# Routing of a mixture-of-experts layer: choice from raw logits, squares from the channel layout, first block gathered by a product on the chip

## The reference, cut to what matters

```
xn2    = rmsnorm(x, norm_ffn_w)               # x * rsqrt(mean(x*x) + 1e-6) * w
logits = xn2 @ router                         # 576 x 8
top_v, top_i = top_k(logits, 2)
gw     = softmax(top_v)
y      = sum over the two experts e of gw[e] * ((silu(xn2 @ w1[e]) * (xn2 @ w3[e])) @ w2[e])
out    = rmsnorm(x + y, norm_final_w)
```

## Time and profile before

| | us |
|---|---|
| median of 3 executions | 2856.9 |
| all three | 2844.24, 2856.9, 2858.02 |
| profiled execution, span from first to last instruction | 2850.7 |
| TensorE matmuls busy | 2468.7 (87%) |
| VectorE busy | 1668.5 (59%) |
| ScalarE busy | 1125.7 (39%) |
| GpSimd busy | 360.3 (13%) |
| mean granted TensorE clock, share of full speed | 0.902 |

### The profile page before, as it was taken

One profiled execution on the slowest core, in us unless ns is written; L12 is line 12 of the kernel. 1 busy time (PEld: TensorE's weight loads), 2 busy tenths in 40 slices (PEclk: granted clock), 3 DMA queues, 4 the chain that ended last, 5 costly groups with the idle time before them and its releaser, 6 DMA issues.

```text
span 2850.7 us, 39807 instructions
## 1 busy us (share of the span) xinstructions
PE 2468.7 (87%) x15802; PEld 2095.7 (74%) x15802; DVE 1668.5 (59%) x1990; ACT 1125.7 (39%) x1370; POOL 360.3 (13%) x160
## 2 busy tenths in 40 slices
PE   5996798698779999969977886979599999999993
PEld 5995686334779999969965863349488888888883
DVE  6853765524423122158627655243689898989895
ACT  4441000453222112134420004532577777777773
POOL 2330000000133333313310000002100000000001
PEclk9997888696889999989978986969799999999997
DMA  4220311300022343122203113001799999999993
GB/s 150 78 61 16 127 53 51 121 23 30 31 96 87 106 149 110 61 94 78 69 16 127 53 51 123 22 30 38 309 420 401 380 381 383 381 387 379 384 376 113
DMA packets 115995, 452.28 MB, mean 159 GB/s; under 512 B 12834, under 2 KB 47522, under 8 KB 86370
## 3 DMA queue, kind: packets, MB, share of 16 engines
q1 hardware_dynamic: 110882, 431.92, 41.3%
q0 software_dynamic: 2624, 9.44, 1.0%
q10 hardware_dynamic: 2304, 8.39, 0.7%
HBM read 415.00 MB, written 42.95 MB: 161 GB/s over the span
## 4 chain that ended last, share of the span: by engine, by line
PE 78%; DVE 12%; ACT 4%; issue 2%; DMA 2%; POOL 1%; another core or an unknown queue 1%; DVEq 0%; SPq 0%; ACTq 0%; POOLq 0%; PEldq 0%
PE ps_buf L508 31%; PE ps_buf L2334 12%; PE ps_buf L2338 6%; PE ps_buf L2365 6%; PE ps_buf L1161 3%; PE ps_buf L2371 3%; PE ps_buf L1196 2%; ACT arena L1735 2%; PE ps_buf L1651 2%; PE ps_buf L1685 1%; PE ps_buf L1149 1%; PE ps_buf L1838 1%; DVE h_buf L572 1%; PE ps_buf L2349 1%; DVE xl_buf L576 1%
## 5 line engine op out<-in xcount | busy, mean ns | idle before, releaser
L508 PE MATMUL ps_buf<-xh_buf,whl_buf 128*128 128x288 f32 x3648 | 663.2, 302 | 76.6 <-POOLq L165 40.5
L2456 DVE TENSOR_TENSOR ring_lo<-ring,high_buf 128x2048 fp32r<-128x2048 f32 (+2 forms) x288 | 594.4, 2108 | 51.7 <-ACT high_buf L2412 49.5
L508 PEld LDWEIGHTS ps_buf<-xh_buf,whl_buf 128*128 128x128 f32 x3648 | 549.6, 192 | 89.5 <-issue 65.0
L2412 ACT CAST high_buf<-ring 128x2048 fp32r<-128x2048 f32 (+2 forms) x288 | 503.0, 1764 | 127.2 <-PE ps_buf L2338 69.0
L508 PE MATMUL ps_buf<-xl_buf,whl_buf 128*128 128x288 f32 x1824 | 398.4, 300 | 0.0
L496 POOL TENSOR_TENSOR whl_buf<-arena,whl_buf 128x1024 fp32r<-128x1024 f32 (+1 forms) x114 | 294.1, 2579 | 602.1 <-ACTq L165 601.5
L493 ACT CAST whl_buf<-arena 128x1024 fp32r<-128x1024 f32 (+1 forms) x114 | 124.7, 1094 | 495.5 <-PE ps_buf L508 476.2
L508 PEld LDWEIGHTS ps_buf<-xl_buf,whl_buf 128*128 128x128 f32 x1824 | 299.0, 193 | 0.0
L2334 PE MATMUL ps_buf<-high_buf,xbh_buf 128*128 128x512 f32 (+1 forms) x768 | 289.8, 377 | 5.3 <-ACT high_buf L2412 5.3
L2334 PE MATMUL ps_buf<-high_buf,xbl_buf 128*128 128x512 f32 (+1 forms) x768 | 288.3, 375 | 0.0
L2338 PE MATMUL ps_buf<-ring_lo,xbh_buf 128*128 128x512 f32 (+1 forms) x768 | 196.1, 377 | 0.0
(11 more groups left out here) (519 smaller groups left out, 3395.8 us busy)
## 6 DMA issues: line engine op xcount, KB each, us to landing
ring<-d_moe_up SPq DMA_DIRECT2D x128, 1024.0 KB, 7.5
ring<-d_moe_dn SPq DMA_DIRECT2D x80, 1024.0 KB, 7.4
ring<-d_moe_up SPq DMA_DIRECT2D x64, 768.0 KB, 6.6
arena<-d_w_in SPq DMA_DIRECT2D x54, 512.0 KB, 3.6
arena<-d_w SPq DMA_DIRECT2D x44, 512.0 KB, 3.6
arena<-d_w SPq DMA_DIRECT2D x16, 704.0 KB, 4.0
arena<-d_pages_c SPq DMA_DIRECT2D x64, 128.0 KB, 2.1
cols_buf<-d_w_out SPq DMA_DIRECT2D x16, 512.0 KB, 3.6
```

The source lines that it names most:

```text
L508: last = nc.tensor.matmul(ps_buf[0:rows, b + a_, 0:HALF], w, m[:, a_ * HALF:(a_ + 1) * HALF], start=start, stop=stop)
L2412: ac.copy(high_part(n), ring[:, 2048 * slot:2048 * slot + unit_cols(n % BLOCK_UNITS)])\
L2456: ve.tensor_tensor(low_part(n), ring[:, at:at + unit_cols(n % BLOCK_UNITS)], high_part(n).bitcast(F32), ALU.subtract).then_inc(S("moe_lo"), 1)
```

## The change: what it does

- **Squares.** They are taken from `x` with channels on the partitions: after each addition VectorE squares the group (128 x 576) and, from the second group on, adds it to a running sum `SQ`. TensorE then sums `SQ` over the partitions with a column of ones, five small products into PSUM. VectorE no longer waits for `XT`, and nothing is left after the loop but the last group.
- **Choice.** The two best experts are taken from the logits before the mean of squares is known. The mean is read between the first and the second choice, and the reciprocal comes after both.
- **Expert numbers** are computed ahead of the slots.
- **Queue of SyncE.** The weight stream no longer waits for the scatters. It waits for them ahead of unit 8 of block 0, and loads block 1 there; block 0 is not loaded from HBM at all. `XN` moves to the last slots of the ring, which unit 8 is the first to touch.
- **Block 0** is gathered on the chip. VectorE builds `HOT` (tokens on the partitions, 128 slots along the row; entry `rstd` where the token's smaller slot is that one, else 0), five instructions that read a row of 1 to 128 from PSUM. TensorE multiplies `XT` by `HOT`, 8 groups of channels by 5 tiles of tokens, fp32. VectorE scales and splits the result in two halves; the first products wait for both halves in turn.
- **Gains** (softmax of the two logits) move behind the first four low parts of block 0.

The core of the diff:

```diff
-        xn_tok = put_at("xn_tok", 5 * D, mx)
+        xn_tok = put_at("xn_tok", 5 * D, mr + RING * 2048 - 5 * D)
@@ wo_dve
-                if sets == 2 and c >= 3:
-                    moe_squares_dve(v, c - 3)
+                if sets == 2:
+                    moe_squares_dve(v, c)
...
-            if sets == 2:
-                for k in range(KD - 3, KD):
-                    moe_squares_dve(v, k)
@@ moe_wo_pe
             moe_turn_pe(KD - 1)
+            pe.matmul(ps_buf[:, 0, 256:256 + P], tb("ones"), tb("rwp")[:, P:2 * P], start=True, stop=True)
+            pe.wait_ge(S("moe_squares"), KD)
+            for i, (t0, n) in enumerate(TILES):
+                last = pe.matmul(ps_buf[0:n, 0, 128 + i:129 + i], SQ[:, 1, t0:t0 + n], tb("ones")[:, 0:1], start=True, stop=True)
+            last.then_inc(S("moe_sums"), 1)
@@ moe_squares_dve
-            ve.wait_ge(S("moe_xt"), k + 1)
-            w = XT[:, :, P * k:P * k + P]
-            v(ve.tensor_tensor(sq_buf[:, 0:5 * P].rearrange("p (i c) -> p i c", i=5), w, w, ALU.mult))
-            v(ve.tensor_reduce(sq_part[:, 5 * k:5 * k + 5], sq_buf[:, 0:5 * P].rearrange("p (i c) -> p i c", i=5), AX.X, ALU.add))
+            if k == 0:
+                v(ve.tensor_tensor(SQ[:, 1, :], x[:, k, :], x[:, k, :], ALU.mult), S("moe_squares"))
+            else:
+                v(ve.tensor_tensor(SQ[:, 0, :], x[:, k, :], x[:, k, :], ALU.mult))
+                v(ve.tensor_tensor(SQ[:, 1, :], SQ[:, 1, :], SQ[:, 0, :], ALU.add), S("moe_squares"))
@@ moe_choose_dve, after the first choice
+                if k == 0:
+                    ve.wait_ge(S("moe_sums"), 1)
+                    v(ve.tensor_scalar(mean2[:, 0:4], ps_buf[:, 0, 128:132], 1.0 / D, 1e-6, ALU.mult, ALU.add))
+                    v(ve.tensor_scalar(mean2[0:64, 4:5], ps_buf[0:64, 0, 132:133], 1.0 / D, 1e-6, ALU.mult, ALU.add), S("moe_mean"))
@@ after both choices
+            ve.wait_ge(S("moe_root"), 1)
+            v(ve.reciprocal(rstd_t, rstd_t), S("moe_rstd"))
@@ after the slots
+            v(ve.tensor_tensor(best, slots[:, 0, :], slots[:, 1, :], ALU.min))
+            for i, (t0, n) in enumerate(TILES):
+                v(ve.tensor_scalar(HOT[0:n, i, :], ps_buf[0:n, 0, 256:256 + P], best[0:n, i:i + 1], rstd_t[0:n, i:i + 1],
+                                   ALU.is_equal, ALU.mult), S("moe_hot"))
@@ moe_sp
-                if b == 0:
-                    sp.wait_ge(S("moe_xs"), 16 * 10)
-                    sp.dma_start(XB[:, 0, :], A["xs"][0:P]).then_inc(S("moe_xb_0"), 16)
...
+                    if b == 0 and u == 8:
+                        sp.wait_ge(S("moe_xs"), 16 * 10)
+                        sp.dma_start(XB[:, 1, :], A["xs"][P:2 * P]).then_inc(S("moe_xb_1"), 16)
@@ new
+        def moe_dispatch_pe():
+            pe = nc.tensor
+            pe.wait_ge(S("moe_xt"), KD)
+            pe.wait_ge(S("moe_hot"), 5)
+            for k in range(KD):
+                for i, (t0, n) in enumerate(TILES):
+                    last = pe.matmul(ps_buf[:, k // 4, P * (k % 4):P * (k % 4) + P], XT[0:n, i, P * k:P * k + P], HOT[0:n, i, :],
+                                     start=i == 0, stop=i == 4)
+                if k == 3:
+                    last.then_inc(S("moe_xbT_half"), 1)
+            last.then_inc(S("moe_xbT"), 1)
@@ moe_dve
-            xbt(0)
+            for h in range(2):
+                ve.wait_ge(S("moe_xbT" if h else "moe_xbT_half"), 1)
+                ks = slice(4 * h, 4 * h + 4)
+                v(ve.tensor_tensor(XBT[:, ks], ps_buf[:, h, 0:512].rearrange("p (k t) -> p k t", t=P),
+                                   nffn[:, ks].unsqueeze(2).to_broadcast([P, 4, P]), ALU.mult))
+                v(ve.tensor_copy(XBH[:, 0, ks], XBT[:, ks]))
+                v(ve.tensor_tensor(XBL[:, 0, ks], XBT[:, ks], XBH[:, 0, ks].bitcast(F32), ALU.subtract),
+                  S("moe_xbt" if h else "moe_xbt_half"))
             lows(0, 0, HIGHS)
+            moe_gains_dve(v)
```

More of the change, by code:

```diff
@@ L275, in build @@
         se_buf = put_at("se_buf", 2 * 512, mc + 2 * E1)
-        sq_buf = put_at("sq_buf", D, mc + 2048)
+        sq_buf = put_at("sq_buf", 2 * T, mc + 2048)
+        hot_buf = put_at("hot_buf", 5 * P, mc + 3264)
         xt_buf = put_at("xt_buf", 5 * D, mc + 4096)
@@ L2074, in build @@
         XT = grid(xt_buf, 0, 5, D)
+        SQ = grid(sq_buf, 0, 2, T)
+        HOT = grid(hot_buf, 0, 5, P)
         XN = grid(xn_tok, 0, 5, D)
@@ L2184, in spread5 @@
                 return ap.unsqueeze(2).to_broadcast([P, 5, 8])
[L2186 to L2187 removed]
             v(ve.memset(lg, 0.0))
+            v(ve.memset(mean2, 1.0))
             ve.wait_ge(S("moe_logits"), 1)
@@ L2191, in moe_choose_dve @@
             v(ve.tensor_copy(lg[0:64, 4, :], ps_buf[0:64, 4, 32:40]))
-            ve.wait_ge(S("moe_root"), 1)
-            v(ve.reciprocal(rstd_t, rstd_t), S("moe_rstd"))
             rank = tb("rrank").rearrange("p (i e) -> p i e", i=5)
@@ L2215, in moe_choose_dve @@
             v(ve.tensor_tensor_scan(last_e, tb("ones")[:, 0:8], blocks_e, 0.0, ALU.mult, ALU.add))
+            w = over[0:1, :].rearrange("p (b e) -> p b e", e=8)
+            v(ve.tensor_tensor(w, tb("blocks", 1).rearrange("p (b e) -> p b e", e=8),
+                               last_e[0:1, :].unsqueeze(1).to_broadcast([1, NBK, 8]), ALU.is_ge))
+            v(ve.tensor_reduce(which[0:1, :], w, AX.X, ALU.add))
+            v(ve.tensor_scalar(ebt_buf[:, :], which[0:1, :], 7.0, None, ALU.min), S("moe_experts"))
             v(ve.tensor_tensor(start_e, last_e, blocks_e, ALU.subtract))
@@ L2223, in moe_choose_dve, with moe_gains_dve @@
             v(ve.tensor_scalar(slot_buf[:, 0:10], slots.rearrange("p k i -> p (k i)"), -1.0, None, ALU.add), S("moe_slots"))
[L2224 to L2228, removed]
+            v(ve.tensor_tensor(best, slots[:, 0, :], slots[:, 1, :], ALU.min))
+            for i, (t0, n) in enumerate(TILES):
+                v(ve.tensor_scalar(HOT[0:n, i, :], ps_buf[0:n, 0, 256:256 + P], best[0:n, i:i + 1], rstd_t[0:n, i:i + 1],
+                                   ALU.is_equal, ALU.mult), S("moe_hot"))
+        def moe_gains_dve(v):
+            ve = nc.vector
             ve.wait_ge(S("moe_exp"), 1)
@@ L2287, in moe_sp @@
                 e = sp.value_load(ebt_buf[0:1, b:b + 1], min_val=0, max_val=7)
-                if b == 0:
-                    sp.wait_ge(S("moe_xs"), 16 * 10)
-                    sp.dma_start(XB[:, 0, :], A["xs"][0:P]).then_inc(S("moe_xb_0"), 16)
-                if b + 1 < NBK:
-                    if b:
-                        sp.wait_ge(S("moe_xbT"), b)
+                if b and b + 1 < NBK:
+                    sp.wait_ge(S("moe_xbT"), b)
                     sp.dma_start(XB[:, (b + 1) % 2, :], A["xs"][P * (b + 1):P * (b + 2)])\
@@ L2323, in moe_up_pe @@
             o = 2 * (gi % 2)
-            if g == 0:
+            if g == 0 and b:
                 pe.wait_ge(S("moe_xbt"), b + 1)
@@ L2328, in moe_up_pe @@
             for q in range(2):
+                if gi == 0:
+                    pe.wait_ge(S("moe_xbt_half" if q == 0 else "moe_xbt"), 1)
                 for w in range(2):
@@ L2375, in moe_pe @@
         def moe_pe():
-            moe_xT_pe(0)
+            moe_dispatch_pe()
             for b in range(NBK):
```

7 lines of the change are left out of this document (3 added, 4 removed).

## The result

The changed kernel takes 2836.83 us (median of nine runs, 2829.76 to 2848.49), the kernel before 2850.12 (nine runs, 2841.14 to 2858.02). The ratio is 0.9953, with an interval of [0.9933, 0.9974]: 13.3 us or 0.47% faster. The interval excludes 1, so the kernel is faster, though by a little less than the 0.5% that I had called the limit of what can be told. The forecast was 2840.9, in a range of 2829 to 2851.

A forecast was written before the change was run, and what follows sets the result against it. TensorE bounds the blocks; routing, scatters and a late weight unit fill the hole ahead of them. 17.0 less 0.9 gave 16 us off the span, 2834.7, and 6.2 above that 2840.9; range 2829 to 2851.

The forecast's parts named there:

- HOT: Five VectorE instructions building the gather's matrix: 0.41 each and a gap of 0.03, 2.2 together, ready at 2004.6.
- The squares and the choice: Routing after the logits: copies start 5.5 us earlier, line 2208 5.36 early, first weights asked for at 2001.2.
- The DMA share: Weights and scatters side by side: scatters get a third of 420 GB/s, 140, and weights 280.
- Rival 2: Weights and scatters together reach 350 GB/s, not 420; unit 8 late by 6 to 7 more; gain 9.5, 2847; chance 0.16.
- the gather of block 0: 80 TensorE instructions after HOT: 11.7 us, with ends of 9.6 and 20.0, finished at 2016.4.
- The clock: During the gather, TensorE starts at clock 0.50 and rises after 4 us: 16 instructions in 4.0, 64 in 7.7.
- The first low part: Unit 0's low part on VectorE waits for the split: 2018.25 + 2.29 = 2020.5, its four products ending at 2021.5.
- The term for unit 8: Unit 8's weights, asked for after the scatters, are ready at 2042.6, wanted at 2041.7: 0.9 late.
- the likeliest case: Whole change: gain of 16 us off the span, with a neighbourhood of 13 to 20; chance 0.64.
- Rival 1: The clock does not rise during the gather: 8.3 lost, less 0.9 of unit 8; gain 8.6, 2848; chance 0.13.
- Rival 3: SyncE's wait for slow scatters holds up unit 8: at 6 us per scatter 14 us slower, 2871; chance 0.07.
- Rival 4: The change doesn't do what it says: the sums wait or VectorE's loop falls behind; no price of its own.

The follow-up runs named there:

- e1: The changed kernel without gather and early weights: SyncE waits for the scatters and loads both blocks before the first unit; 2843.52 us, ratio 0.9993.
- e8: The changed kernel with low parts between the split's halves, scatter wait moved to unit 14, 2 and 15 idle products around the count; 2835.56 us, ratio 0.9946.
- e4: The changed kernel with idle TensorE products, 10 ahead of the count and 30 behind it; 2837.98 us, ratio 0.9968.
- r_after: The changed kernel run again with no edit; 2840.1 us, ratio 0.9955.
- e3: The changed kernel with low parts of units 0 and 1 between the split's halves and the gather in other PSUM banks; 2841.13 us, ratio 0.9964.
- e5: e3 with idle TensorE products, 4 before the count and 36 after it; 2842.12 us, ratio 0.996.
- e6: e5 with SyncE's wait for the scatters moved from unit 8 to unit 14 and the scattered rows outside those ring slots; 2836.11 us, ratio 0.9943.
- e2: e1 with units 0 to 7 asked for first and the scatter wait and both block loads ahead of unit 8; 2861.66 us, ratio 1.0042.

## Why the prediction was right, and where its sizes were off

**Right, to a few tenths.** The squares and the choice: the copies at 0.11 after the logits' end (forecast 0.1), the sum of both picks at 3.82 (3.77), the first weights at 8.31 (8.3), the scatters at 9.79 (9.6). By e1 the part is worth 4.8 in the stretch, where the step's 5.36 less the 0.84 for the experts is 4.5. HOT: 0.40 to 0.42 each, as read off between the two forms of the earlier trace rows (0.41), with a gap of 0.15 and not 0.03: 2.6 for the five, not 2.2. HOT ran beside scatters, kept the interpolated 0.41, and the scatters kept their pace (first to last issue 11.44 before, 11.45 after). The section "SBUF: two separate sides" of the Trainium skill (SBUF — State Buffer) gives the lock a condition that I had left out: on VectorE's side it takes an instruction in a two-port mode or one with two inputs from SBUF. HOT has one input tensor, in PSUM, and the trace agrees with the section in that nothing was locked. And I had read the row wrongly: the 1.13 is the first scatter's in every run, in e1 too, where VectorE is idle beside it, and the second and third, beside HOT, take 0.96 and 0.95. With two inputs from SBUF it is another matter. In e8 the last scatter stands beside a low part:

```profile
2020.41 2.73 POOL L2268 DMA_INDIRECT d_xs<-xn_tok,slot_buf  x1 [0.30 <-issue]
```

2.73 where it takes 0.90 in the other kernels.

The DMA share: from 2000 to 2020 the queues show, packets, MB and share:

```profile
q1 hardware_dynamic: 770, 5.65, 67.4%
q0 software_dynamic: 750, 2.74, 33.5%
```

As many packets on either side, and so twice the bytes for rows twice as long; I had taken 2:1 from the earlier trace rows, where another engine's queue stood beside the weights. The page "DMA: Bandwidth & Descriptors" of the Trainium skill, section "Queues, rings and completion order", says that a DMA engine goes round its queues packet by packet; the 770 and 750 agree. From this I had 42.6 for the last landing; it came at 43.0. Rival 2 (350 GB/s for both together) falls by the 422 to 426 in the stretches above.

**The step that failed in size: the gather of block 0.** The forecast put 11.7 us for 80 instructions, from 0.12 at full clock, 0.25 at the lower one, and 4 us until the clock rises. Measured: 14.95 and 14.03. Two terms:
- The pace at full clock. I took a row of 8 instructions in 1.06, less the drain of the last, 0.12 each. For tiles of 128 rows that was right, even a little high (0.112 in e4, in the gather and in the idle products alike). But I priced all 80 instructions by that form, and 16 of them belong to the tile of 64 tokens: e4 and e8 have 80 in 12.07, 2.5 us over the 9.6 that I had. Five tiles of up to 128 tokens for 576 tokens are named before the prediction, and the trace of before had the price of the change of form. That the range's end of 9.6 was not an end at all is the worst of it.
- The clock. It rose 6.3 us after the work began in the profiled run and 4.3 in r_after, where I had 4. With the 12.07 known, the low clock cost 2.9 and 2.0, where the forecast had 2.1 (11.7 less 9.6).

It started 0.8 late (12.63, forecast 11.8: HOT's gaps and the routing's 0.2), ran 3.3 longer, and unit 0 was used up at 33.53, not 28.6.

**A wait that I had on the path but whose echo I missed.** The first low part is behind both splits, so TensorE idles 2.38 before it. I priced the wait. I did not ask what the clock does in it: in the profiled run it fell, and 1.6 more went in units 0 and 1 (1.56 for r_after's 1.20, 3.06 for 1.84). In r_after it did not fall.

**The term for unit 8.** 0.9 late in the forecast, nothing in the result, because TensorE itself came 5 us later than I had it. e3, e5 and e6 show the term: 2.6 lost when TensorE is earlier, 5.3 given back when the wait moves.

Together, for the profiled run: 17.0 at unit 0's use, less 0.8 (start) and 3.3 (gather) gives 12.9; the split and the clock's relapse take 0.8 to unit 0, 12.1 measured, and 1.2 in unit 1: 10.9. In r_after without the relapse 13.0 at unit 0, 12.7 at block 1. The mechanism of the likeliest case was the right one, at two thirds to four fifths of its size (10.9 to 12.7, of 16), and so just under the 13 to 20 that I had called its neighbourhood. The measured gain in time, 13.3 us with an interval of 7.4 to 19, agrees with either. That the span after, 2833.0, came within 1.7 of the forecast's 2834.7 is luck: 7.1 of its 17.7 is the earlier end of the logits.

**Two errors that met.** I put 6.2 us around the profiled span, taking its execution for the median. In all nine runs of the changed kernel time and span are 2.2 to 2.4 apart. With 2.3 the profiled execution of before was one of 2853.0 (worked out, not shown by a row), and the forecast's gain of 16 off that is 2837.0. The median of before's nine runs is 2850.12; less the stretch's 10.9 to 12.7 it gives 2837.4 to 2839.2, and 2836.83 was measured. So the forecast of 2840.9 stood on a base 6.8 above the median before (2856.9 against 2850.12) and a gain 3 to 5 too large, and these partly cancel: that it missed by only 4.1 is in part luck. A median of three runs that lie 13.8 apart was too weak a base, and the range had to carry it.

**The rivals.** Rival 1 (the clock stays low): no, the windows show it rising, but part of its price was paid. Rival 3 (slower): no, the scatters were asked for at their old pace and landed at 43.0, not after 60. e2 is slower in another way, with scatters that land at 42.4 and a block 0 that needs them. Rival 4: no, every step stands at its place.

## What to carry to other kernels

A wait that holds two things back must be priced for the pair: against e1, taking the weights out from behind the scatters alone cost 15 us, taking block 0's rows out alone gave 1.7, both gave 6 to 8. Where TensorE is asked to do a small job after idling, take the pace from rows of every form that occurs in it, the short last tile and the steps to and from it too, and reckon the low clock for longer than the shortest rise seen; then ask what the next short wait does to the clock again. And where the upstream spreads by more than the gain, anchor both traces at the last event ahead of the edit and at the first behind it, and compare that stretch.

## What the runs showed that I had not expected

- **A busy TensorE whose clock falls.** In e4 the ten idle products came right behind the logits (products of 8 columns) and the five sums (1 column). TensorE was busy 2.00 of 2 us in 1988 to 1990 and in 1990 to 1992, and the granted clock was 0.72 and then 0.50. In e5 and e8 it was at 0.50 when the products behind the count began. What made it fall is not shown.
- **The same wait, two answers.** After 2.38 us of idling ahead of the first low part the clock fell in the profiled run, and after 2.37 us it did not in r_after. That is 1.6 us between two executions of one kernel.
- **The spread goes with the clock.** Over the nine runs of the changed kernel the span goes with the mean granted clock: 2827.5 and 2828.3 at 0.910, 2832.9 to 2834.8 at 0.907 and 0.908, 2837.5 at 0.906, 2842.7 at 0.904, 2846.1 at 0.902. The logits' end moved by 18 us between executions (1985.77 to 2003.84) on the same code, while the part behind block 1 stayed within 766.9 to 767.5, where TensorE hardly idles. What sets the clock's course in the first 2000 us was not studied and stays open.
